# The low parts of the down product's weight sums: VectorE in place of GpSimd, each next to its high part

## The reference

```python
def swiglu(h, w_gate, w_up, w_down):
    return (jax.nn.silu(h @ w_gate) * (h @ w_up)) @ w_down

x = x + jnp.concatenate([mix, cross], axis=-1) @ w_out[i]
x = x + swiglu(rms_norm(x, ffn_norm[i]), w_gate[i], w_up[i], w_down[i])
```

## Time and profile before

| | |
|---|---|
| time, median of 3 runs | 1380.42 us (1380.15 to 1380.5) |
| time of the profiled execution | 1380.77 us |
| its span, first to last instruction | 1379.0 us |
| mean granted TensorE clock | 0.993 |
| busy: PE, VectorE, ScalarE, GpSimd | 97%, 75%, 50%, 31% |
| low parts B on GpSimd (L1461) | 70 instructions, 93.7 us |
| loop of bodies, first down step to last | 778.5 to 1353.5 us |

### The profile page before, as it was taken

One profiled execution on the slowest core, in us unless ns is written; L12 is line 12 of the kernel. 1 busy time (PEld: TensorE's weight loads), 2 busy tenths in 40 slices (PEclk: granted clock), 3 DMA queues, 4 the chain that ended last, 5 costly groups with the idle time before them and its releaser, 6 DMA issues.

```text
span 1379.0 us, 20577 instructions
## 1 busy us (share of the span) xinstructions
PE 1337.9 (97%) x6854; PEld 1092.8 (79%) x6854; DVE 1041.1 (75%) x1218; ACT 689.1 (50%) x1206; POOL 421.0 (31%) x309
## 2 busy tenths in 40 slices
PE   7999999999999999699999999999999999999999
PEld 4877888887878888577887878888888888888887
DVE  5677978897887988786338878768787787877865
ACT  7676666666566666674235343333433334334341
POOL 1000000000000000214013956547465474754631
PEclk9999999999999999799999999999999999999999
DMA  7100101100010101103301221221212112121103
GB/s 244 31 24 17 39 16 32 30 22 23 23 30 23 30 23 39 31 24 105 117 1 39 84 69 34 75 62 38 68 30 72 59 44 68 30 68 49 58 31 122
DMA packets 90469, 69.92 MB, mean 51 GB/s; under 512 B 4144, under 2 KB 75824, under 8 KB 90416
## 3 DMA queue, kind: packets, MB, share of 16 engines
q1 hardware_dynamic: 90416, 69.24, 16.3%
HBM read 65.03 MB, written 4.19 MB: 50 GB/s over the span
## 4 chain that ended last, share of the span: by engine, by line
PE 91%; ACT 3%; DVE 3%; POOL 1%; issue 1%; DMA 0%; SPq 0%; ACTq 0%; POOLq 0%; DVEq 0%
PE ps L1298 27%; PE ps L326 18%; PE ps L1473 14%; PE ps L1009 7%; PE ps L380 6%; PE ps L364 5%; PE ps L354 4%; PE ps L295 3%; PE ps L1086 2%; PE ps L1528 2%; PE ps L797 1%; ACT junk L702 1%; PE ps L937 1%; PE ps L901 0%; PE ps L737 0%
## 5 line engine op out<-in xcount | busy, mean ns | idle before, releaser
L1483 DVE TENSOR_TENSOR x<-ps,x 128x2048 f32<-128x2048 f32 x70 | 160.2, 2289 | 97.6 <-PE ps L1473 97.6
L565 POOL TENSOR_TENSOR o_t<-o_t,pv_low 128x256 f32 x24 | 23.6, 985 | 477.3 <-ACT o_t L461 477.3
L1266 DVE TENSOR_TENSOR part_l<-part_x,part_h 128x512 fp32r<-128x512 f32 x140 | 142.0, 1038 | 28.4 <-POOL part_x L1244 19.7
L1461 POOL TENSOR_TENSOR bl<-bx_B,bh 128x512 fp32r<-128x512 f32 x70 | 93.7, 1338 | 199.2 <-ACT bh L1457 199.2
L449 ACT ACTIVATE a_h<-ps 128x256 fp32r<-128x256 f32 (+2 forms) x96 | 78.0, 813 | 136.9 <-PE ps L364 136.9
L326 PE MATMUL ps<-hh,w_h 128*128 128x512 f32 x336 | 140.3, 418 | 0.0
L326 PE MATMUL ps<-hh,w_l 128*128 128x512 f32 x336 | 132.3, 394 | 0.0
L326 PE MATMUL ps<-hl,w_h 128*128 128x512 f32 x336 | 131.9, 393 | 0.0
L558 DVE TENSOR_TENSOR a_l<-ps,a_h 128x256 fp32r<-128x256 f32 (+2 forms) x96 | 91.5, 953 | 49.0 <-ACT a_h L449 48.6
L1298 PE MATMUL ps<-ft_h,part_l 128*128 128x512 f32 x320 | 126.5, 395 | 0.0
L1298 PE MATMUL ps<-ft_l,part_h 128*128 128x512 f32 x320 | 125.2, 391 | 0.0
(11 more groups left out here) (277 smaller groups left out, 3431.2 us busy)
## 6 DMA issues: line engine op xcount, KB each, us to landing
w_raw<-in_sb_w_in SPq DMA_DIRECT2D x52, 256.0 KB, 2.9
bx_B<-in_w_down SPq DMA_DIRECT2D x44, 256.0 KB, 3.0
part_x<-in_w_gate SPq DMA_DIRECT2D x40, 256.0 KB, 2.9
part_x<-in_w_up SPq DMA_DIRECT2D x40, 256.0 KB, 2.9
wo_raw<-in_w_out SPq DMA_DIRECT2D x20, 256.0 KB, 2.7
x_in<-in_x SPq DMA_DIRECT2D x8, 512.0 KB, 8.3
x<-in_x SPq DMA_DIRECT2D x16, 256.0 KB, 5.1
out<-x SPq DMA_DIRECT2D x16, 256.0 KB, 2.0
```

The lines of the kernel that those rows point to most:

```text
L1266: dve.tensor_tensor(part_l[m][p][:, :, :].rearrange(flat), part_x[m][p][:, :, :].rearrange(flat), part_h[p][:, :, :].rearrange(flat).bitca ...
L1461: pool.tensor_tensor(bl[(par + k) % 2][:, :], bx[B_OPS[k]][:, :], bh[(par + k) % 2][:, :].bitcast(F32), ALU.subtract).then_inc(s_bw, 1)
L1483: dve.tensor_tensor(o, ps[:, 0:4], o, ALU.add).then_inc(s_x2, 1)
```

## The change

`pool_b_low` becomes `dve_b_low`: the same subtraction with the same waits and the same semaphore, issued by VectorE. In `dve_body` low part k stands right ahead of `dve_a_low` k, for k = 1 to 6 of the body's chunk and, at the end, for k = 0 of the next. The very first one moves from ahead of the loop on GpSimd to ahead of `dve_a_low(0, 0, 0)` on VectorE. Nothing else moves.

```diff
-        def pool_b_low(pool, c, par, k):
-            pool.wait_ge(s_bh, 7 * c + k + 1)
-            pool.tensor_tensor(bl[(par + k) % 2][:, :], bx[B_OPS[k]][:, :], bh[(par + k) % 2][:, :].bitcast(F32),
-                               ALU.subtract).then_inc(s_bw, 1)
+        def dve_b_low(dve, c, par, k):
+            dve.wait_ge(s_bh, 7 * c + k + 1)
+            dve.tensor_tensor(bl[(par + k) % 2][:, :], bx[B_OPS[k]][:, :], bh[(par + k) % 2][:, :].bitcast(F32),
+                              ALU.subtract).then_inc(s_bw, 1)
...
         def pool_body(pool, c, par, ahead=True):
             pool_a_sum(pool, c, par, 3)
-            pool_b_low(pool, c, par, 1)
-            pool_b_low(pool, c, par, 2)
             pool_b_sum(pool, c, 2)
             pool_b_sum(pool, c, 3)
             pool_sums(pool, c + 1, 1)
-            pool_b_low(pool, c, par, 3)
             pool_last_sum(pool, c + 1, 1)
-            for k in (4, 5, 6):
-                pool_b_low(pool, c, par, k)
             if ahead:
                 pool_sums(pool, c + 2, 0)
                 pool_b_sum(pool, c + 1, 0)
-                pool_b_low(pool, c + 1, 1 - par, 0)
                 pool_last_sum(pool, c + 2, 0)
                 pool_b_sum(pool, c + 1, 1)
...
+            dve_b_low(dve, c, par, 1)
             dve_a_low(dve, c, par, 1)
             if not first:
                 dve_down(dve, c, 0)
...
             if ahead:
                 dve_down(dve, c, 6)
+                dve_b_low(dve, g, par1, 0)
                 dve_a_low(dve, g, par1, 0)
...
-            pool_b_low(pool, 0, 0, 0)
             pool_sums(pool, 1, 0)
...
             dve_first(dve, 0, 1)
+            dve_b_low(dve, 0, 0, 0)
             dve_a_low(dve, 0, 0, 0)
```

More of the change, by code:

```diff
@@ L1636, in dve_body @@
             dve_part_low(dve, g, 0, 6)
+            dve_b_low(dve, c, par, 2)
             dve_a_low(dve, c, par, 2)
@@ L1639, in dve_body @@
             dve_sum(dve, g, 0, par1, 1)
+            dve_b_low(dve, c, par, 3)
             dve_a_low(dve, c, par, 3)
@@ L1644, in dve_body @@
             dve_sum(dve, g, 0, par1, 2)
+            dve_b_low(dve, c, par, 4)
             dve_a_low(dve, c, par, 4)
@@ L1649, in dve_body @@
             dve_part_low(dve, g, 1, 4)
+            dve_b_low(dve, c, par, 5)
             dve_a_low(dve, c, par, 5)
@@ L1655, in dve_body @@
             dve_part_low(dve, g, 1, 6)
+            dve_b_low(dve, c, par, 6)
             dve_a_low(dve, c, par, 6)
```

## The result

| | before | after |
|---|---|---|
| median of the runs | 1380.53 us (6 runs) | 1385.27 us (6 runs, 1384.35 to 1386.71) |
| time of the profiled execution | 1380.77 us | 1384.35 us |
| its span | 1379.0 us | 1382.6 us |

The ratio is 1.0033, with a 95% interval of 1.0023 to 1.0044: 4.7 us slower. Later the changed kernel was measured once more, with ten runs: 1384.75 us, ratio 1.0025 (1.0015 to 1.0034). The profiled execution is the fastest of its six. I account for its span, 3.6 us longer than that of the profiled execution before.

A forecast was written before the change was run, and what follows sets the result against it. PE (TensorE) was taken to bound the kernel. Nine stalls of 0.66 us (+5.9) less 0.6 in body 0 gave +5.3 us on a median of 1380.42, forecast as 1385.8 us, range 1379.6 to 1390.2.

The forecast's parts named there:

- PE has nothing to gain in the loop: Feed-forward loop, 879 to 1353 us: PE busy 474.00 of 474.00 us, so relieving other engines gives nothing back.
- The loop, and that it closes nine times: PE step 6, VectorE addition and low part, five GpSimd sums, VectorE addition 0, PE step 1; bodies 1 to 9, +5.9 us.
- The size of a stall: PE's wait before step 1, starting at 962.43 against 961.77 before: 0.66 us in each of nine bodies.
- Body 0: First loop body: part lows run alone, addition 1 comes earlier and PE's 0.61 us wait at 796 goes, -0.6 us.
- Costed at nothing: Low parts 1 to 6 in the loop: later sums and loads stay hidden; low part 2 with 1 us of cover.
- The sums fit: Rival: GpSimd's five sums take 7.34 us with two disturbed, so no stall at step 1; 1379.8 us, chance 0.24.
- Full blocking: Rival: four GpSimd sums each stretched by the full 0.60 us, stall 1.32 nine times; 1391.7 us, chance 0.08.
- VectorE falls behind: Rival: low part 2's chain delays addition 2, up to 1 us more in each of nine bodies; 1394 us, chance 0.04.

## Why the prediction was right

It gave 1385.8 us in a range of 1379.6 to 1390.2, and slower with 0.75. Measured were 1385.27 and 1384.75.

- *PE has nothing to gain in the loop:* right. The kernels without stalls win only what PE lost in body 0 and ahead of it.
- *The loop, and that it closes nine times:* right in every link. Low part 0 at 2.21 after addition 6 (forecast 2.20), GpSimd 0.76 after it (0.78), the sums 8.06 to the end of the last (8.13), addition 0 at 11.67 (11.82), PE's step 2.34 after it (2.42). The loop came out at 14.01 or 14.08 us, in alternate bodies (13.99 in the first of the nine and 14.17 in the last), where the forecast had 14.24. The experiments show the links one by one: where low part 0 stands, what stands behind B-sum 1, and how many VectorE instructions stand beside the sums.
- *The size of a stall:* 0.66 forecast, 0.58 on average. Two errors partly cancel: the loop was 0.2 too long, and I left out the 0.1 that PE loses on the matmul after a wait. Nine stalls are 5.2 in place of 5.9.
- *Body 0:* -0.6 forecast, -0.9 measured, for the reason forecast: the two part lows take 1.28 us (785.72) in place of 3.48, and addition 1 starts at 789.33. The size was too small, as I counted the shown idle time of the earlier trace rows and not the starts. The low part ahead of the loop, costed at nothing, gave 0.1.
- *Costed at nothing:* low parts 1 to 6 cost nothing. L1244 starts at 972.32 (about 974 forecast), addition 2 at 974.72. The late load of B22 is there, 1.8 us on average ahead of L1435, and hidden. A low part 6 made twice changed nothing.
- *The sums fit:* wrong as it stood, since four sums were disturbed and not two. That it decides by this count was right: with fewer VectorE instructions beside them the sums took 7.14 us and did fit.
- *Full blocking:* wrong. GpSimd's disturbed instructions follow each other after 1.59, 1.64 or 1.70 us, against 1.25 undisturbed: a stretch of 0.34 to 0.45, not 0.60. By the rule of the Trainium skill, page "SBUF — State Buffer", section "Who interferes with whom", the second to issue is shut out for the whole of the first; measured on this side it is less. On VectorE's side the trace nearly agrees: behind a GpSimd instruction of 1.25 us that had begun 0.07 before, low part A 1 took 1.76 in place of 0.69.
- *VectorE falls behind:* wrong. It is busy for 84% of the 474 us, as forecast, and no wait of PE but that for addition 0 appeared. The time given for this rival was also added up wrong: nine times 1 us on top of 1385.8 is 1394.8, not 1394.

## What to carry to other kernels

Before an instruction is moved, list who waits for its semaphore and what stands behind that waiter in its queue; then follow the list until it meets the bounding engine or ends. Here a subtraction of 0.6 us held five sums, and the last of them held the addition that PE wanted; an engine that is idle for a quarter of the time is no protection against that. Once such a loop is found, it can be opened at any of its links. Three did it here: the producer ahead of the addition, the waiter behind three of the sums, and less work beside the sums.

## What the runs showed of the hardware that was not expected

- A wait of PE costs about 0.1 us more than its length: the second matmul after it starts 0.33 or 0.34 us after the first, not 0.23, in eight of the nine stalls, and 0.31 in the last.
- Between VectorE and GpSimd a lead of 0.07 us was enough: low part A 1 took 0.69 us with GpSimd idle, and 1.76 behind a GpSimd instruction that had begun 0.07 us before.
- The additions (L1483, one input in PSUM) took 2.28 us each, whatever GpSimd did beside them.
